# Two transformer blocks in one kernel: attention heads taken in pairs, and the softmax division on another engine

## The reference, cut

```python
def first_block(x, ...):                       # 256 tokens, width 1024
    x = x + 0.5 * rmsnorm(swiglu(rmsnorm(x, g0), ...), g1)
    q, k, v = (rmsnorm(x, g2) @ w_qkv)         # 16 heads of 64
    o_na  = neighbourhood_attention(q[:8], k[:8], v[:8], rel_bias)
    o_dil = dilated_mixture_attention(q[8:], k[8:], v[8:], t5_bias)
    x = x + rmsnorm(concat(rmsnorm(o_na), rmsnorm(o_dil)) @ w_out, g3)
    return x + 0.5 * rmsnorm(swiglu(rmsnorm(x, g4), ...), g5)

def second_block(x, c, ctx, ...):
    for l in range(2):                         # in layer 0 the context of 256 tokens too
        h = rms_norm(x, norm1_g[l]) * (1 + scale) + shift     # modulation(c, w_mod[l])
        q, k, v, ... = split(h @ w_in[l])      # 8 heads of 64, 2 key/value heads
        logits = concat([s_win, s_ctx, sink])  # 256 window keys, 256 context keys, one sink
        p = jax.nn.softmax(logits, axis=-1)    # exp(s - max) / sum
        o_a = p[keys] @ v
        y = merge_branches(fourier_mix(...), o_a, hgrn_readout(...), gates, ...)
        x = x + gate * (y @ w_out[l])
        x = x + gate * sq_relu_mlp(adaln_norm(x), w_ff1[l], w_ff2[l])
    return x
```

## Time and profile before

| | |
|---|---|
| median of 3 runs | 2095.09 us (2094.78 to 2096.33) |
| the profiled execution | 2094.94 us, its span 2093.1 us |
| granted clock over the span | 0.988 |
| PE busy | 2007.8 us (96%) |
| DVE busy | 1267.9 us (61%) |
| ACT busy | 944.5 us (45%) |
| POOL busy | 433.4 us (21%) |
| chain that ended last | PE 79%, DVE 10%, ACT 5% |

### The profile page before, as it was taken

How to read it: one execution, slowest core, us unless ns; L and a number is a source line. 1 busy time by engine, 2 the same in 40 slices (tenths; PEclk the granted TensorE clock), 3 DMA queues, 4 the chain that set the end, 5 groups by cost and what they waited for, 6 DMA issues and landing times.

```text
span 2093.1 us, 30363 instructions
## 1 busy us (share of the span) xinstructions
PE 2007.8 (96%) x12246; PEld 1756.3 (84%) x12246; DVE 1267.9 (61%) x1962; ACT 944.5 (45%) x1493; POOL 433.4 (21%) x270
## 2 busy tenths in 40 slices
PE   7999899899989999999999999999989899998999
PEld 6899887899978888787688788888878898697999
DVE  5678797778855863543863583354365946776410
ACT  5444445555446333323653542243265453655643
POOL 1201000000000000000044554555500000002887
PEclk9999999999999999999999999999999999999999
DMA  7987461566722112211023344466522333144554
GB/s 254 273 295 263 159 234 41 180 223 229 264 91 95 60 48 91 91 61 61 1 81 111 109 150 143 149 202 202 181 88 94 101 121 111 51 141 142 182 191 151
DMA packets 84636, 299.22 MB, mean 143 GB/s; under 512 B 9993, under 2 KB 13201, under 8 KB 84113
## 3 DMA queue, kind: packets, MB, share of 16 engines
q1 hardware_dynamic: 64512, 231.76, 32.3%
q0 software_dynamic: 17280, 60.95, 9.1%
q10 hardware_dynamic: 2704, 4.57, 0.6%
HBM read 296.18 MB, written 4.11 MB: 143 GB/s over the span
## 4 chain that ended last, share of the span: by engine, by line
PE 79%; DVE 10%; ACT 5%; issue 3%; DMA 3%; ACTq 0%; POOL 0%; DVEq 0%; POOLq 0%
PE ps L458 21%; PE ps L453 21%; PE ps L456 21%; DVE wl L436 3%; DMA wr<-wstream 2%; ACT wh L420 2%; PE ps L1601 1%; PE ps L538 1%; PE ps L982 1%; PE ps L984 1%; PE ps L987 1%; PE ps L1042 1%; PE ps L1059 1%; PE ps L1082 1%; PE ps L1039 1%
## 5 line engine op out<-in xcount | busy, mean ns | idle before, releaser
L453 PE MATMUL ps<-HH,wh 128*128 128x256 f32 (+1 forms) x2336 | 766.8, 328 | 22.8 <-ACT HH L1320 10.7
L458 PE MATMUL ps<-HH,wl 128*128 128x256 f32 (+1 forms) x2336 | 753.5, 323 | 7.2 <-DVE wl L436 6.0
L456 PE MATMUL ps<-HL,wh 128*128 128x256 f32 (+1 forms) x2336 | 752.1, 322 | 0.5 <-DVE HL L1334 0.4
L420 ACT ACTIVATE wh<-wr 128x1024 fp32r<-128x1024 f32 x440 | 461.2, 1053 | 387.1 <-PE ps L458 333.5
L436 POOL TENSOR_TENSOR wl<-wr,wh 128x1024 fp32r<-128x1024 f32 x143 | 355.8, 2493 | 993.5 <-ACT wh L420 992.6
L436 DVE TENSOR_TENSOR wl<-wr,wh 128x1024 fp32r<-128x1024 f32 x297 | 361.8, 1227 | 246.8 <-ACT wh L420 244.4
L453 PEld LDWEIGHTS ps<-HH,wh 128*128 128x128 f32 x2336 | 449.1, 192 | 67.3 <-issue 28.7
L458 PEld LDWEIGHTS ps<-HH,wl 128*128 128x128 f32 x2336 | 448.9, 192 | 43.1 <-DVE wl L436 9.3
L456 PEld LDWEIGHTS ps<-HL,wh 128*128 128x128 f32 x2336 | 449.2, 192 | 36.9 <-issue 2.4
L458 PE MATMUL ps<-HIDH,wl 128*128 128x512 f32 (+1 forms) x512 | 173.1, 338 | 0.0
L453 PE MATMUL ps<-HIDH,wh 128*128 128x512 f32 (+1 forms) x512 | 172.8, 338 | 0.0
(11 more groups left out here) (255 smaller groups left out, 2604.1 us busy)
## 6 DMA issues: line engine op xcount, KB each, us to landing
wr<-wstream SPq DMA_DIRECT2D x440, 512.0 KB, 3.3
WM<-wmod POOLq DMA_DIRECT2D x68, 512.0 KB, 4.0
X<-wmod POOLq DMA_DIRECT2D x28, 512.0 KB, 5.4
NAB<-naskew POOLq DMA_DIRECT2D x16, 128.0 KB, 12.6
dilskew<-lines POOLq DMA_DIRECT2D x1, 2048.0 KB, 20.8
DILB<-dilskew POOLq DMA_DIRECT2D x2, 1024.0 KB, 13.5
COND<-cond ACTq DMA_DIRECT2D x2, 1024.0 KB, 5.9
CT<-consts POOLq DMA_DIRECT2D x1, 1216.0 KB, 9.5
```

What stands on the lines that cost most here:

```text
L420: ins = e.activation(self.WH[i % NSPL][:, :], self.WR[n % NRAW][:, :], ACT.Copy)
L453: e.matmul(out, wh, xh, start=i == 0, stop=False)
L456: e.matmul(out, wh, xl, start=False, stop=False)
L458: ins = e.matmul(out, wl, xh, start=False, stop=i == n_k - 1)
```

## The change

It has three parts.

1. **Pairs.** Units are taken two by two, one on the lower and one on the upper half of the array (in the layers the order of units is changed so that neighbours lie on different halves). The scores of a pair are issued matmul by matmul in turn, and so are its values, which write different halves of the output tile. At odd t the scores of t+1 and t+2 stand behind the transposes of t-2, then the fill, then the values of t-3 and t-2; at even t there are only the transposes and the fill. ACT's order in a step is unchanged.
2. **The multiply by the reciprocal** is POOL's (`pool_units`, L1199): for block 1 behind the bias loads, for layer 0 behind the 20 loads of the second half of its modulation, for layer 1 behind the loop of layer 0's feed-forward. On DVE the sink is added by an instruction for each group of rows (L1181).
3. **Layer 1's output product.** ACT makes the high half one block ahead of the square. On DVE the low half of d+1 stands behind x_new of d.

```diff
@@ layer_units @@
     for j in range(4):
-        for kv in range(2):
-            for a in range(2):
+        for a in range(2):
+            for kv in range(2):
...
+    def pe_scores(self, e, w, pair, S, qk):
...
+        parts = [self.score_parts(u) for u in pair]
+        for i in range(len(parts[0])):
+            for u, part in zip(pair, parts):
+                a, b, queries, keys = part[i]
+                ins = e.matmul(self.aux.item(("s", u.key))[:, a:b], queries, keys, start=True, stop=True)
...
+    def pe_values_of(self, e, w, pair, P, v_there):
...
+        for u in pair:
+            w.wait_ge(*self.c("u_pt").at(u.key))
...
+        for i in range(4):
+            for u, part in zip(pair, parts):
+                at, values, c, start, stop = part[i]
+                ins = e.matmul(b[u.off:u.off + 64, at:at + 128], values, P.item(u.key)[:, c:c + 128], start=start, stop=stop)
...
@@ pe_units @@
         for t in range(-1, n + 3):
-            if t + 1 < n:
-                u = units[t + 1]
...
             if 2 <= t <= n + 1:
                 u = units[t - 2]
                 P.take(u.key)
...
+            if t % 2 and t + 1 < n:
+                self.pe_scores(e, w, units[t + 1:t + 3], S, qk)
             fill()
-            if t >= 3:
-                u = units[t - 3]
...
+            if t % 2 and 3 <= t <= n + 1:
+                self.pe_values_of(e, w, units[t - 3:t - 1], P, v_there)
...
@@ dve_units @@
                 if u.kind != "b1":
-                    e.tensor_tensor(den, den, st[:, 6:6 + rows], ALU.add).then_inc(*self.c("u_den").mark(u.key))
+                    for i in range(rows):
+                        ins = e.tensor_scalar(den[:, i:i + 1], den[:, i:i + 1], st[:, 6 + i:7 + i], None, ALU.add)
+                    ins.then_inc(*self.c("u_den").mark(u.key))
                     w.wait_ge(*self.c("u_den").at(u.key))
                 e.reciprocal(den, den).then_inc(*self.c("u_inv").mark(u.key))
-                w.wait_ge(*self.c("u_inv").at(u.key))
-                ins = e.tensor_tensor(sv, sv, bc(den, 2, 512 // rows), ALU.mult)
-                ins.then_inc(*self.c("u_p").mark(u.key))
-                self.st.release(u.key, self.c("u_p"), u.key)
...
+    def pool_units(self, e, w, units, rings):
+
+        for u in units:
+            rows, st = u.rows, self.ST[:, self.st.item(u.key), :]
+            sv = rings[0].item(u.key)[:, :].rearrange("p (r k) -> p r k", r=rows)
+            w.wait_ge(*self.c("u_inv").at(u.key))
+            ins = e.tensor_tensor(sv, sv, bc(st[:, 4:4 + rows], 2, 512 // rows), ALU.mult)
+            ins.then_inc(*self.c("u_p").mark(u.key))
+            self.st.release(u.key, self.c("u_p"), u.key)
...
@@ act_add_out @@
+        ahead = 1 if key == ("out", 1, 0) else 0
         for d in range(8):
-            self.make_high(e, w, *self.steps(key + (d,), ks))
+            for n in range(d + ahead if d else 0, min(d + ahead + 1, 8)):
+                self.make_high(e, w, *self.steps(key + (n,), ks))
             if squares:
                 self.act_square(e, w, key, d, self.X[:, d, 0:T], [self.c("x_new").at(key + (d, T // 256 - 1))])
...
@@ dve_add_out @@
+        by_dve = key == ("out", 1, 0)
+        if by_dve:
+            self.make_low(e, w, "lo_dve", (key + (0,), 0))
         for d in range(8):
             k = key + (d,)
-            if key == ("out", 1, 0):
-                self.make_low(e, w, "lo_dve", (k, 0))
...
             self.main.release(k, self.c("x_new"), k + (T // 256 - 1,))
+            if by_dve and d < 7:
+                self.make_low(e, w, "lo_dve", (key + (d + 1,), 0))
...
@@ pool @@
         self.pool_bias_loads(e, w)
+        self.pool_units(e, w, block1_units(), self.unit_rings(1))
...
             self.pool_mod(e, w, 0, 1, ch)
+        self.pool_units(e, w, layer_units(0), self.unit_rings(2))
...
+        self.pool_units(e, w, layer_units(1), self.unit_rings(2))
         self.make_low(e, w, "lo_pool", *self.steps(("ff2", 1, 0, 7), range(32)))
```

More of the change, by code:

```diff
@@ L1021, in unit_sink, with score_parts @@
         return self.vec("attn_sink_2", 8 * l + u.head)
+    def score_parts(self, u):
+        rows, j = slice(u.off, u.off + 64), u.j
+        if u.kind == "x":
+            return [(0, 512, self.Q2[rows, j, 128 * u.a:128 * u.a + 128], self.K2[rows, :])]
+        if u.kind == "b1":
+            return [(256 * a, 256 * a + 256, self.QT[rows, j, 128 * a:128 * a + 128], self.KT[rows, j, :]) for a in range(2)]
+        return [(256 * a, 256 * a + 256, self.Q2[rows, j, 256 + 128 * a:384 + 128 * a], self.K2[rows, 256:512])
+                for a in range(2)]
@@ new lines, in value_parts @@
+    def value_parts(self, u):
+        if u.kind == "x":
+            return [(128 * u.a, self.V2[:, c, u.off:u.off + 64], 128 * c, c == 0, c == 3) for c in range(4)]
+        if u.kind == "b1":
+            return [(128 * a, self.VR[:, k, 64 * u.head:64 * u.head + 64], 256 * a + 128 * k, k == 0, k == 1)
+                    for a in range(2) for k in range(2)]
+        return [(128 * a, self.V2[:, 2 + c, u.off:u.off + 64], 256 * a + 128 * c, c == 0, c == 1)
+                for a in range(2) for c in range(2)]
@@ new lines, in pe_scores @@
+    def pe_scores(self, e, w, pair, S, qk):
+        for u in pair:
+            S.take(u.key)
+            self.st.take(u.key)
+            self.aux.take(("s", u.key))
+            for x in self.aux.before(("s", u.key)) + qk(u):
+                w.wait_ge(*x)
+        parts = [self.score_parts(u) for u in pair]
[3 more added lines that the diff above has]
+                ins = e.matmul(self.aux.item(("s", u.key))[:, a:b], queries, keys, start=True, stop=True)
+                if i == len(part) - 1:
+                    ins.then_inc(*self.c("u_score").mark(u.key))
@@ new lines, in pe_values_of @@
+    def pe_values_of(self, e, w, pair, P, v_there):
+        group = pair[0].group
+        if pair[0].first:
+            self.main.take(group)
+            for x in self.main.before(group):
+                w.wait_ge(*x)
+        b = self.main.item(group)
+        for u in pair:
+            w.wait_ge(*self.c("u_pt").at(u.key))
+            for x in v_there(u):
+                w.wait_ge(*x)
+        parts = [self.value_parts(u) for u in pair]
+        for i in range(4):
+            for u, part in zip(pair, parts):
+                at, values, c, start, stop = part[i]
+                ins = e.matmul(b[u.off:u.off + 64, at:at + 128], values, P.item(u.key)[:, c:c + 128], start=start, stop=stop)
+                if i == 3:
+                    ins.then_inc(*self.c("u_pv").mark(u.key))
+                    P.release(u.key, self.c("u_pv"), u.key)
@@ L1026, in pe_units @@
         for t in range(-1, n + 3):
-            if t + 1 < n:
-                u = units[t + 1]
-                S.take(u.key)
-                self.st.take(u.key)
-                self.aux.take(("s", u.key))
-                b, off, j = self.aux.item(("s", u.key)), u.off, u.j
-                for x in self.aux.before(("s", u.key)):
-                    w.wait_ge(*x)
-                for x in qk(u):
-                    w.wait_ge(*x)
-                if u.kind == "b1":
-                    for a in range(2):
-                        ins = e.matmul(b[:, 256 * a:256 * a + 256], self.QT[off:off + 64, j, 128 * a:128 * a + 128],
-                                       self.KT[off:off + 64, j, :], start=True, stop=True)
-                elif u.kind == "x":
-                    ins = e.matmul(b[:, :], self.Q2[off:off + 64, j, 128 * u.a:128 * u.a + 128],
-                                   self.K2[off:off + 64, :], start=True, stop=True)
-                else:
-                    for a in range(2):
-                        ins = e.matmul(b[:, 256 * a:256 * a + 256],
-                                       self.Q2[off:off + 64, j, 256 + 128 * a:384 + 128 * a],
-                                       self.K2[off:off + 64, 256:512], start=True, stop=True)
-                ins.then_inc(*self.c("u_score").mark(u.key))
             if 2 <= t <= n + 1:
```

27 lines of the change are left out of this document (removed).

## The result

The changed kernel takes **2109.9 us** (median of 4 runs, 2107.46 to 2112.88) against 2095.71 for the kernel before: ratio 1.0069, 95% interval 1.0051 to 1.0086. It is slower by 0.7%, where 2098.0 and no measurable change were forecast; the range of 2090 to 2110 held the median by 0.1 us. The profiled execution has a span of 2111.1 us, 18.0 more than before.

A forecast was written before the change was run, and what follows sets the result against it. TensorE, busy for 96% of the span, was taken to bound the kernel. Block 1 -2.7, layer 0 +6.5, layer 1 +4.1 and output product -5.0 summed to +2.9: 2098.0 us against the median, 8-in-10 range 2090 to 2110.

The forecast's parts named there:

- The clock: TensorE's granted clock: taken as 1.00; losing it was named only as what would make the forecast wrong, without a chance.
- The window ring: Layers' window pairs: next scores wait for the pair's masks, sum, multiply and transposes; 6.19 us a pair, before 5.32.
- Block 1's ring: Block 1's pairs: next scores wait through masks, reciprocal, multiply and transposes; 5.57 us a pair, before 5.32.
- The multiply on POOL: Each unit's 128x512 multiply, moved from DVE: 1.30 us taken, outer bounds 0.69 and 2.41.
- The overlap: Pairs on different array halves: window scores 2.12 to 1.59, block 1's and context's to 1.33, values 2.04 to 1.15.
- The Fourier steps: Layer 0's window pairs with Fourier halves: 8.17 us, being 6.19 plus 0.69 and about 0.30 of waiting each step.
- Starts and tails: Stretches' ends: fifth unit's scores at 306.04, 986.16, 1793.95; behind the last scores 10.0, 11.1 and 10.3 us.
- The three stretches: Attention units of block 1, layer 0 and layer 1: changes of -2.7, +6.5 and +4.1 us.
- The output product: Layer 1's output product: column blocks 2.83 us apart instead of 3.45, giving -5.0 us at L605.
- Held small instructions: Rival: POOL's multiply also stops DVE's two-column negations and the reciprocals, over 0.3 a pair; about 2105.4 us, chance 0.24.
- No overlap: Rival: the array halves don't overlap in scores and values, +11.6 to the sum; about 2109.6 us, chance 0.18.
- Faster: Rival: multiply 1.20, no small gaps or holds, shorter tails, layers' ring 5.9; about 2090.5 us, chance 0.16.

The follow-up runs named there:

- TensorE kept busy: The changed kernel with unread matmuls of 128x256 ahead of units' transposes and three ahead of each window pair's values; 2099.3 us.
- the version with early scores: The changed kernel with a pair's scores issued ahead of the transposes of unit t-2 instead of behind them; 2079.84 us.
- the last version: The changed kernel with pair scores ahead of the transposes and unread matmuls at long waits, seven ahead of block 1's first values; 2069.71 us.
- window pairs on one half: The changed kernel with each head's matmuls issued in a row and both window units of a pair on the same array half; 2118.3 us.

## Why the prediction was wrong

It forecast a net of +2.9 us and got +14 by the medians, +18.0 in the profiled executions. The step that failed is the clock: the sum priced every ring, start and tail at the 1.00 of before and put the loss of clock at nothing, though the change takes a quarter of TensorE's work in the stretches away. The granted clock fell to 0.92, 0.80 and 0.98, and by the run with TensorE kept busy that cost about 10.1 us of the 15.1 between +2.9 and +18.0. With the clock kept, as in that run, the three stretches still come to +13.2 where +7.9 was summed. By the prediction's own steps:

- **The clock** (a term put at nothing). The prediction named TensorE's loss of its clock as what would make it wrong, and gave it no price and no chance. It was worth about 10 us, most of the miss: 2098.0 + 10 is 2108.
- **The window ring** (right). Where it closes, through which instructions, and the starts within it agree within 0.04 us up to the reciprocal. At full clock it was 5.82 against 6.19: 0.26 because the multiply took 1.04 and not 1.30, 0.11 because it started sooner.
- **Block 1's ring** (the size right by luck). 5.56 to 5.65 against 5.57, but with a multiply 0.26 shorter and the way to the reciprocal 0.32 longer, most of it the held negation. In a context ring, 6.30 against 6.27, a negation takes 0.51 us in place of 0.23.
- **The multiply on POOL** (term mis-sized). 1.30 allowed for a fixed part; 1.04 is below half of the instruction twice as wide. The Trainium skill (GPSIMD Engine Reference, "3.1 Elementwise — side-by-side cycle accounting") gives 4497 ns for 2048 fp32 elements; a quarter of it, an estimate, is 1.12, and the trace shows 1.04. That would have been nearer than the 1.30.
- **The overlap** (term mis-sized, nearly harmless). Scores of different heads overlap entirely, 2.12 becomes 1.06 and not 1.33 or 1.59. It hardly mattered, since the ring sets the pair; taking the overlap away in window pairs lengthened the ring by 0.12.
- **The Fourier steps** (terms wrong). 8.17 a pair was the ring plus twice DVE's subtraction (0.69) and twice a hold (0.30). At full clock one such pair of layer 0 took 7.42 (996.54 to 1003.96 with TensorE kept busy; the one before it, 8.35, began at half clock), 1.60 more than the plain ring. The changed kernel's own rows, in a ring that starts at 1000.69, show where that comes from:

```profile
1004.44 0.62 ACT L2091 ACTIVATE HH<-FR 128x512 fp32r<-128x512 f32 x1
1004.96 0.38 ACT L1110 ACTIVATE s<-ps 128x256 f32<-128x256 f32 x1
1005.10 0.69 DVE L2097 TENSOR_TENSOR HL<-FR,HH 128x512 fp32r<-128x512 f32 x1 [1.05 <-ACT HH L2091]
...
1006.55 0.41 DVE L1164 SCALAR_TENSOR_TENSOR s<-ps,CT 128x256 f32<-128x256 f32 x1
```

ACT's high half stands once ahead of the second side copy (2.16 after the first one and not 1.65: 0.5), and DVE's subtraction once ahead of the maximum and the second mask (1.59 behind the copy and not 0.50: 1.1). Only one of the two subtractions is in the ring, ACT's work was left out, and there was no hold: L2097 takes 692 ns on average, as L2081 did before.

- **Starts and tails** (terms mis-sized). With the clock kept, the tails are 12.0, 12.6 and 12.0 and not 10.0, 11.1 and 10.3, together 5.2 us; the held L1272 is a part of it in block 1, and what makes the layers' longer no run took apart. The way to the third pair is 2.9 longer in all: already ahead of its scores TensorE waits for POOL (2.58 us in layer 0 of the changed kernel), where the sum had nothing but work. The pairs between are 2.8 shorter.
- **The three stretches.** With the clock kept they are +1.6, +7.4 and +4.2, forecast -2.7, +6.5 and +4.1. That the layers come so near is luck: shorter pairs and longer starts and tails cancel. In block 1 nothing cancels, and the sign was wrong. The changed kernel's first ring there took 7.48 and not 6.2: the copy to `VR` cost what was allowed, but DVE also makes a low half of weights (L436, 1.23 us) ahead of the first mask, which comes 2.11 after the scores and not 1.24, and the clock was low.
- **The output product** (right). -5.0 forecast, -6.4 and, alone, -6.2 measured.
- **The rivals.** Held small instructions: the mechanism is there, by the means 0.15 us in a pair of block 1 and 0.35 in one of the context, where the rival asked for over 0.3; only one negation of a pair stands in the ring, the reciprocals were not held (163 ns in the median, 164 before), and a block 1 ring of 6.34 is not seen. No overlap: refuted, though its 2109.6 us is the time that was measured; the number agrees by chance. Faster: its multiply was nearer, and the time was on the other side.

So the change's three parts are one gain (part 3), one that is worth nothing in the order of before and nothing clear in pairs as they stand (part 2), and one that costs (part 1): pairs behind the transposes close a ring and give up the slack that the old order had.

## What to carry over

When several steps of a pipeline are grouped, write down which later instruction of each engine the group's first one now waits for, in that engine's own order: a ring that closes once a group costs more than the work that the grouping saves, and moving one call can open it. Work taken off the engine that sets the pace buys idle time, and idle time on TensorE has a price of its own; put a price and a chance on the clock wherever a change takes a quarter of TensorE's time away. Move work to the slower engine only after asking whether the place has slack: the same multiply was worth 0 and 8 to 10 us in two orders.

## What the runs showed of the hardware

- Matmuls of 64 rows on different halves of the array overlap entirely in scores (eight records in 1.13 us, four on one half in 1.13), also when all of one half's stand ahead of the other's (1.14). Values overlap entirely only when dealt out in turn: 1.09 us, 1.55 head after head, 1.93 on one half.
- POOL's multiply of 128x512 takes 1.04 us, less than half of the 1024-wide subtraction's 2.41, and 1.20 where DVE's subtraction with two SBUF inputs runs beside it; that one goes from 0.43 to 1.26.
- Beside that multiply DVE's negations of two columns take longer (0.39 for 0.17 us in block 1's pairs), those of one column do not: 0.21 us at 1838.82, inside a multiply that lasts from 1838.26 to 1839.30.
- The clock falls to its lower level in work that waits again and again: in the changed kernel behind a wait of 2.58 us in layer 0, and in the version with early scores behind one of 3.68:

```profile
311.66 1.60 PE L1074 MATMUL ps<-p,VR 128*64 128x128 f32 x16 [3.68 <-ACT p L1130]
313.19 1.11 PE L1094 MATMUL ps<-CT,s 128*128 128x128 f32 x4
```

These values take 1.60 and the transposes 1.11, where full-clock ones take 1.09 and 0.66. With seven unread matmuls in that wait the values behind it take 1.09 (at 308.14 in the last version). The length of one wait does not tell: in layer 0 of the changed kernel the values behind a wait of 1.93 us ran at full clock at 1012.10 and 1024.60 (1.09 and 1.10 us), and at 1017.92 took 1.54, with the lower clock behind them. A busier TensorE (window pairs on one half) still lost its clock in layer 0.
